# RWKV-7 recurrence in 64-token chunks on 64x64 tiles, two units interleaved, results taken by two engines; preparation without centring, transposes inside it

## What is computed

```python
def rwkv7_scan(r, decay, k, v, kk, a):
    B, S, H, N = r.shape
    b = kk * a

    def step(state, inp):
        r_t, w_t, k_t, v_t, kk_t, b_t = inp
        sa = jnp.einsum('bhvk,bhk->bhv', state, -kk_t)
        state = (state * w_t[:, :, None, :] + sa[..., None] * b_t[:, :, None, :]
                 + v_t[..., None] * k_t[:, :, None, :])
        y = jnp.einsum('bhvk,bhk->bhv', state, r_t)
        return state, y
```

## Time and profile before

| | us |
|---|---|
| median of 3 runs | 4273.46 (4272.99 to 4274.66) |
| profiled execution | 4271.92 |
| its span, first to last instruction | 4270.0 |
| from the end of the attention to the first solve matmul | 92.9 |
| from there to the end of the solve | 245.0 |

### The profile page before, as it was taken

One profiled execution on the slowest core, in us unless ns is written; L12 is line 12 of the kernel. 1 busy time (PEld: TensorE's weight loads), 2 busy tenths in 40 slices (PEclk: granted clock), 3 DMA queues, 4 the chain that ended last, 5 costly groups with the idle time before them and its releaser, 6 DMA issues. The chain is left out here.

```text
span 4270.0 us, 46461 instructions
## 1 busy us (share of the span) xinstructions
PE 3190.7 (75%) x16422; PEld 1593.8 (37%) x16422; DVE 2527.2 (59%) x6260; ACT 864.6 (20%) x2369; POOL 1164.1 (27%) x1028
## 2 busy tenths in 40 slices
PE   4976388779367566598879996698879886666666
PEld 3853288444123111163345551353345551111111
DVE  5557766432874677745744558645744458855554
ACT  1113200110121111213622111123622111111111
POOL 0000000000344344432323334232323334444443
PEclk9997698889678777796789997796989997766666
DMA  4520000111799999998889999696889999999998
GB/s 177 180 82 1 6 1 1 47 61 67 304 402 414 371 412 419 402 394 316 307 323 385 373 367 383 260 392 238 298 329 389 355 367 416 409 420 417 418 420 359
DMA packets 201655, 1246.97 MB, mean 292 GB/s; under 512 B 24461, under 2 KB 28813, under 8 KB 66965
## 3 DMA queue, kind: packets, MB, share of 16 engines
q0 software_dynamic: 147456, 1073.81, 62.7%
q1 hardware_dynamic: 53976, 170.32, 10.8%
HBM read 1239.54 MB, written 4.46 MB: 291 GB/s over the span
## 5 line engine op out<-in xcount | busy, mean ns | idle before, releaser
L232 POOL DMA_INDIRECT held_pair<-in_experts,held_expert x1024 | 1163.9, 1137 | 3078.4 <-PE held_acc L252 1867.9
L252 PE MATMUL held_acc<-held_pair,held_diag 64*64 64x512 f32 x8192 | 1411.7, 786 | 602.0 <-ACT held_diag L278 563.4
L298 DVE CUSTOM_DVE_ANT_0 held_pair<-held_pair,held_hrow 128x1024 f32<-128x1024 f32 x1024 | 1248.6, 1223 | 779.4 <-DMA held_pair<-in_experts,held_expert 771.0
L252 PEld LDWEIGHTS held_acc<-held_pair,held_diag 64*64 64x64 f32 x8192 | 270.6, 158 | 1470.3 <-ACT held_diag L278 1254.9
L278 ACT ACTIVATE held_diag<-held_bands,held_weight 128x64 f32<-128x64 f32 x1024 | 347.8, 340 | 1424.0 <-DVE held_weight L293 1389.2
L271 ACT ACTIVATE held_bent<-held_dot 128x2 f32<-128x2 f32 x512 | 104.0, 203 | 747.9 <-DVE held_dot L298 719.7
L1605 PE MATMUL c_ps<-held_hT,c_w 128*128 128x256 f32 (+1 forms) x480 | 148.9, 465 | 0.0
L617 PE MATMUL pgh_ps<-held_hT,pgh_w 128*128 128x256 f32 x608 | 141.2, 385 | 0.0
L617 PE MATMUL p2h_ps<-held_hT,p2h_w 128*128 128x256 f32 x576 | 133.9, 386 | 0.0
L1649 DVE COPY held_room<-c_ps 128x256 f32<-128x256 f32 (+1 forms) x48 | 24.6, 513 | 178.7 <-PE c_ps L1605 178.7
L617 PEld LDWEIGHTS pgh_ps<-held_hT,pgh_w 128*128 128x128 f32 x608 | 112.4, 190 | 43.0 <-issue 28.4
...
## 6 DMA issues: line engine op xcount, KB each, us to landing
...
held_pair<-in_experts,held_expert POOLq DMA_INDIRECT x1024
...
```

Of the source, the lines that this page charges most:

```text
L232: pool.indirect_dma_start(self.pair[m % BUFS][:], None, self.layers[t // TT][0], bass.IndirectOffsetOnAxis(ap=self.expert[:, t % TT, s:s + ...
L252: last = pe.matmul(self.sum_of(i)[to * BAND:(to + 1) * BAND], diag[band, :], up[band, turn * WIDE:(turn + 1) * WIDE], start=s == 0, stop=s ...
L298: ins = dve.tensor_tensor_reduce(down, down, self.hrow[:, t % TT, :], 1.0, 0.0, ALU.mult, ALU.add, self.dot[:, t % 2, s:s + 1])
```

## The change

**Preparation.** The squares are summed by 8-column weights into 8 rows, one per head (`rows`); VectorE takes the maximum, ScalarE the root, VectorE the reciprocal of 8x512, and four matmuls with `pick` spread the rows to 128 partitions again, from where VectorE multiplies them into `kk`. The scans are four of 512 tokens, restarted at each 64 by a zero in `again`. Nothing is centred; two exponentials in place of three, and the shifted one is read from its neighbour column. Two more products, `bend` and `kend`, carry the decay to the end of the chunk. The sixteen transposed groups and the bonus are made in the same stage; ScalarE takes them out of PSUM. Twelve of them go where the exponentials stood, so ScalarE begins them after `kkd_made` has reached 2.

**Solve.** The unit is 128 tokens as before, but holds two chunks of 64. Each matrix is 64x64; the matrices of the first chunk of a unit lie in partitions 0 to 63 and those of the second in 64 to 127. The steps 16, 18 and 19 are gone. A job is a step, a unit and a half of the heads (`part`); its matmuls alternate over `e`, and both halves write to the same bank, on different partitions. `solve_order` interleaves two units: u0 part 0, u0 part 1, u1 part 0, u1 part 1, then the next step. State steps (RATE, GROW, WITHIN, STATE, ACROSS) follow, and STATE and ACROSS of a pair are put between the first steps of the next. ScalarE takes the results of the steps in `BY_ACT`, VectorE the others; TensorE waits for exactly the results that a job needs, and for the job eight before it, whose bank it takes. There are 200 jobs. GpSimd makes one product, `decays`, for which VectorE waits ahead of its first result.

```diff
-def rwkv_prepare_stage(nc, k, z, g, cols, hT, KR, rk, sgate, mid_e, end_e):
+def rwkv_prepare_stage(nc, k, z, g, cols, hT, KKd, Rd, rk, sgate, dend, vT, kkT, bT, kdT, bonus):
...
+        units = [(src, dst, m) for src, dst in ((vz, vT), (bend, bT), (KKd, kkT), (kend, kdT)) for m in range(RP)]
...
-                for m in range(4):
-                    pe.matmul(ps[m][:], pair_ones[:], c[:, m, :], start=True, stop=True).then_inc(norms, 1)
+                for m in range(RP):
+                    last = pe.matmul(ps[0][0:8, :], sums[:, 8 - 2 * m:16 - 2 * m], c[:, m, :], start=m == 0, stop=m == RP - 1)
+                last.then_inc(summed, 1)
+                for n in range(3):
+                    turn(n)
...
+                for m in range(RP):
+                    pe.matmul(ps[SPREAD[m]][:], pick[:, m, :], rows[:], start=True, stop=True).then_inc(spread, 1)
...
+                act.activation(eneg, c[:], ACT.Exp, scale=DECAY).then_inc(exps, 1)
+                act.activation(einc, c[:], ACT.Exp, scale=-DECAY).then_inc(exps, 1)
...
+                act.wait_ge(kkd_made, 2)
+                for n in range(4, 16):
+                    keep(n)
...
+                dve.wait_ge(summed, 1)
+                link(dve.tensor_scalar(rows[:], ps[0][0:8, :], 1e-24, None, ALU.max))
+                dve.sem_inc(floored, 1)
+                for m in range(RP):
+                    ins = dve.tensor_tensor_scan(c[:, m, :], again[:], ld[:, m, :], 0.0, ALU.mult, ALU.add)
...
+                dve.reciprocal(rows[:], rows[:]).then_inc(inverted, 1)
+                for m in range(RP):
+                    dve.wait_ge(spread, m + 1)
+                    dve.tensor_tensor(kk[:, m, :], kk[:, m, :], ps[SPREAD[m]][:], ALU.mult).then_inc(used, 1)
...
-                link(dve.reciprocal(eprev[:], eprev[:]))
...
-                c3, ld3 = c[:].rearrange("p m (t n) -> p (m t) n", n=P), ld[:].rearrange("p m (t n) -> p (m t) n", n=P)
-                link(dve.tensor_copy(mid_e[:], c3[:, :, P // 2 - 1]))
-                ins = dve.tensor_tensor(c3, c3, bcast(mid_e[:], P, 2), ALU.subtract)
...
-def rwkv_turn_stage(nc, k, z, g, KR, rk, kkT, bT, kdT, vT, bonus):
...
-def rwkv_solve_stage(nc, k, g, KR, Bd, Kd, kkT, bT, kdT, vT, mid_e, end_e, y):
...
+CH = 64
+UNITS = S // P
...
+POWERS = (0, 1, 2, 3, 4, 5, 6, 7, 8, 9, 10, 11, 12, 20, 13, 14, 15, 17, 21, 22)
+RATE, GROW, WITHIN, STATE, ACROSS = 23, 24, 25, 26, 27
+BY_ACT = (5, 6, 8, 9, 11, 13, 15, 20, 21, 22, GROW, WITHIN)
...
+def solve_order(units):
+
+    pairs = [units[i:i + 2] for i in range(0, len(units), 2)]
+    waiting = []
+    for pair in pairs:
+        for step in POWERS:
+            for u in pair:
+                yield step, u, 0
+                yield step, u, 1
+            for job in waiting[:2]:
...
+            @block.gpsimd
+            def _(pool):
+                pool.wait_ge(loaded, 32)
+                pool.tensor_tensor(decays[:], bcast(ident[:], RP * S // CH, 1), bcast(dend[:], CH, 2), ALU.mult).then_inc(decays_made, 1)
...
+                for n, (step, u, part) in enumerate(order):
+                    s = u % 2
+                    ps = bank[n % 8]
+                    if n >= 8:
+                        after(order[n - 8])
+                    if step <= 4:
+                        half = rows(part)
+                        for m in range(RP):
+                            for e in range(2):
+                                seg = slice(u * P + e * CH, u * P + e * CH + CH)
+                                lhs, rhs = {0: (Bd, KKd), 1: (KKd, Bd), 2: (Kd, KKd), 3: (Bd, Rd), 4: (Kd, Rd)}[step]
+                                last = pe.matmul(ps[rows(e), lane(m)], lhs[half, m, seg], rhs[half, m, seg], start=True, stop=True)
...
+                        for m in range(RP):
+                            for e in range(2):
+                                h = 4 * part + m
+                                last = pe.matmul(ps[rows(e), lane(m, width)], lhs[s][rows(e), h, :], rhs[s][rows(e), h, :], start=True, stop=True)
...
+                    elif step == STATE:
+                        after((RATE, u, part))
+                        if part:
+                            after((STATE, u, 0))
+                        elif u:
+                            after((STATE, u - 1, 1))
```

454 lines of the change are left out of this document (258 added, 196 removed).

## The result

The changed kernel takes 4121.79 us (median of 4 runs, 4112.01 to 4125.93), the kernel before 4273.23 us (4 runs, 4261.17 to 4274.66): a ratio of 0.9648, 95% interval 0.9624 to 0.9673. That is 151 us less. The sign and the main term of the forecast were right, the size was not: 4154 had been forecast, with 4130 as the lower end of the range.

The account below looks back on a forecast made before the run. A serial preparation and solve, the solve bound mainly by TensorE, limits the kernel. Solve 114.5 + 7.7 + 2.4 + 5 + 2.4 + 3.6 = 135.6 us, ending at 654.8 for 773.9: 119.1 us gained, 4154 us forecast, range 4130 to 4240.

Parts of the forecast that it names:

- What bounds it, and the sign: Stretch from attention's end through the recurrence: nothing else runs, TensorE busy 215.6 of the solve's 245.0 us; forecast faster, 0.91.
- (2) The row sums: Preparation: four matmuls summing squares run at 1.2 GHz, 1.71 us each, 6.8 us that VectorE waits for.
- The middle: Preparation after the row sums: scans 4.6, product 2.3, reciprocal 3.3 us, to 482.2; norms spread by 489.4.
- The large products: Preparation on VectorE after the norms are spread: five large products of 2.29 us, everything through at 507.1.
- The transposed blocks: End of preparation: ScalarE's last twelve copies, 7.1 us, start only after VectorE's products at 507.1; end set at 514.7.
- (3) GpSimd: Start of solve, first matmul at 518.9: GpSimd's product takes 4.6 us (nothing to 9), hidden behind 20 jobs, 17 us.
- (4) A matmul of 64x64x64: Solve: 60 ns a matmul at 2.4 GHz because two tiles stream at once; 114.5 us with the 128-column ones.
- Steps 0 to 4 of the first pair: Start of solve: first 20 jobs at 1.2 GHz, 0.86 us each, 17 us; 7.7 us extra, 2.4 until the clock rises.
- Second pair's steps 0 to 4: Mid-solve: about 5 us extra, as VectorE's 28 results (9.5 us) take as long as TensorE's 9.6 us.
- The rest: Norm, merge and experts after the solve: unchanged, starting earlier, so the whole gain of 119.1 us stays.
- the low clock throughout: Rival: solve stays at 1.2 GHz, 216 us for 135.6, kernel 4235 us; chance 0.16.
- half or missing overlap: Rivals, solve: tile pairs overlap partly (4195 us; 0.13 with other small costs) or not at all (4435 us; 0.07).

Follow-up runs that it names:

- e_prep_warm: Changed kernel plus nine unread 128x128 by 512 matmuls before the preparation's norm-spreading matmuls; preparation 77.7 us for 77.9, solve 120.6 us.
- e_late_decays: Changed kernel with VectorE waiting for GpSimd's product only before its first RATE result; first pair's steps 0 to 4 8.9 us for 10.5, solve 2.2 us shorter.
- m_supply: Changed kernel plus four long rows of wait-free matmuls after the last solve job; 64-column rows: 50.8 ns a matmul on four tiles, 65 on two.
- t_four_tiles_all: Changed kernel with all four tiles taking turns in steps 5 to 22 and WITHIN too, output wrong; steps 5 to 17 took 25.0 us for 24.6.
- the second time: Unedited changed kernel measured again beside the kernel before: 4117.84 us (5 runs), ratio 0.9661.

## Why the prediction was right or wrong

The mechanism of the gain was right, and two steps of the sum failed most: the price of a job in steps 0 to 4 (0.86 and 0.48 us, put by its own two tiles, measured 0.49 and 0.33), and the rest of the kernel, whose scatter was put at nothing. In the order of the steps; the sum of the differences is the miss.

- **What bounds it, and the sign**: right. The stretch is serial, TensorE bounds the solve, and its gain went through to the end.
- **(1) Up to the sigmoids**: 463.46 for 464.24, 0.8 us earlier. Right.
- **(2) The row sums**: the step "At 1.2 GHz such a matmul takes 2 x 0.855 = 1.71" failed. They took 3.60 us for 6.8: their clock was 2.4 GHz, granted from 461.6 on, behind the 64-row matmuls; I had carried over the level of the matmuls before. It is not a constant either: with the same instructions it fell again between 464.1 and 465.0 in seven of the fourteen profiles, as in e_prep_warm, and took 5.30 us there. So 3.60 us in the profile that was compared is in part luck. The trace of the kernel before had the same sign: its clock rose at 461.2, within the stretch that I had taken for 1.2 GHz, and fell at 464.6.
- **The middle**: floor, scans, first product and reciprocal end at 478.2, the spread at 486.2, each 4 us early by the row sums (3.2) and the earlier start (0.8); their own terms (4.6, 2.3, 3.3, 7.2) were right.
- **The large products**: I counted five, the code has six (L1121 to L1130): 1.9 us too little.
- **The transposed blocks**: "Only now may ScalarE take the last twelve" named the wrong gate. The exponentials are last read at L1127, not at L1130, so the copies began at 502.75, beside the last product. Last copy 509.5 for 514.7. With the start of the solve (3.3 us for 4.2) the first matmul came at 512.83, 6.1 us before the forecast: 16.1 us gained for 10.
- **(3) GpSimd**: the product cost 3.61 us, within its bounds; the Trainium skill's 4497 ns (page "GPSIMD Engine Reference", 3.1 Elementwise) is above what this trace shows. "Even 9 us are hidden" was wrong: e_late_decays gives 2.2 us. The argument went by job 21, but the ninth job already needs the bank of the first, which VectorE must have emptied: eight jobs of 0.86 us would hide 6.9 us at most. With jobs of 0.3 to 0.5 us the eight were through by 516.7, when VectorE had just taken its first result (516.12 to 516.54). From there VectorE set the pace, and its three operations for each result of step 1 held the thirteenth to the fifteenth job 1.0 us apart.
- **(4) A matmul of 64x64x64**: 58.2 ns for 60. Right, and so were steps 5 to 22: 31.8 us a pair for 33.5. The reason given, two tiles at a time, is half of it: m_supply shows the supply of instructions at the same 58.3 ns. Each of the two alone would give this pace (two tiles take half of 109 ns at least, and t_four_tiles_all had four tiles and was no faster), so which of them holds the changed kernel can't be told from these runs; that 60 ns came out is in this part luck.
- **Steps 0 to 4 of the first pair**: the largest miss, 10.5 us for 19.7. Two terms failed. The clock rose at 516.2, after 3.4 us, and not after 20 jobs. And a job took 0.49 us at 1.2 GHz and 0.33 at 2.4 (0.29 in e_late_decays, where VectorE sets the pace later), for 0.86 and 0.48: the two jobs of a unit stand on different row halves, TensorE reads ahead from one into the other, and all four tiles work. I had priced a job by its own two tiles. Jobs that came alone, because VectorE held them back, show the two-tile pace:

```profile
518.58 0.68 PE L1235 MATMUL rsolve_bank<-rwkv_Rd,mix_z 64*64 64x64 f32 x16 [0.31 <-DVE rsolve_T L1363]
...
516.76 1.51 PE L1235 MATMUL rsolve_bank<-rwkv_KKd,mix_z 64*64 64x64 f32 x60
```

((0.68 - 0.22) / 15 = 31 ns a record in the first, (1.51 - 0.22) / 59 = 22 in the second.) A third term was put at nothing: the waits for VectorE, which hold three jobs 1.0 us apart.

- **RATE and GROW** for the same reason: with WITHIN 10.3 and 10.5 us for 11.5. **Second pair's steps 0 to 4**: 16.0 us for 18.4. VectorE was the bound, as put; that TensorE's clock would fall in the pause (574.3 to 581.1) was not. **The last STATE jobs**: 7.8 for 7.7.
- **The rest**: "I expect the whole gain to stay" is not contradicted as a mean, and fails as a bound. Behind the solve the same code takes 3476.7 to 3502.1 us in the fourteen profiles; before had 3496.1, the changed kernel 3489.4. The 6.7 us between these two are within that scatter, whose mean is 3488.7. There is one profile of the kernel before, so a true difference of a few us in the rest is not excluded: the medians differ by 151 us and, the second time, by 148, for 142 at the end of the solve, which both intervals still include. I set the range's lower end from the solve and the preparation alone, 14 us and 115 us, and gave this scatter nothing. With the preparation at 16.1, beyond its bound, 4121.8 lay 8 us outside. Most of those 8 us are that scatter: without the 6.7 us the profiled run would have taken 4129.9.

In sum: 6.1 (preparation) + 17.1 (solve, 9.2 of it in steps 0 to 4 of the first pair) + 6.7 (rest) = 29.9 us, of 29.6 between 4152.8 and 4123.17. Of the rivals, neither the low clock throughout nor the half or missing overlap happened; none of them was on the fast side, and that was the gap in the list.
